# Dilated attention computed as a near part and a far part, joined per pair of heads

## The chip, the core and the metric

The program runs on one core of one Trainium2 chip. Its engines work side by side, each through its own instructions in order: TensorE (PE) multiplies matrices into PSUM banks, VectorE (DVE) and ScalarE (ACT) do elementwise work, GpSimd (POOL) splits weights, SyncE (SP) issues most DMAs. Engines wait for one another through semaphores. The metric is the device time of one execution in microseconds; lower is better.

## The reference, cut to what matters

The program is a decoder trunk of two layers at 1024 positions and width 1024, in fp32. The change touches one part of layer 0: attention with 8 heads of width 64, in which three dilated windows are mixed.

```python
DILATED_BRANCHES = ((128, 1), (512, 4), (2048, 16))   # (window, dilation)

def dilated_attention(q, k, v):
    outs = [dilated_branch(q, k, v, w, d) for (w, d) in DILATED_BRANCHES]
    ms = jnp.stack([m for _, m, _ in outs])
    ls = jnp.stack([l for _, _, l in outs])
    os_ = jnp.stack([o for o, _, _ in outs])
    wts = ls * jnp.exp(ms - jnp.max(ms, axis=0, keepdims=True))
    o = jnp.einsum('gbhs,gbhsd->bhsd', wts, os_) / jnp.sum(wts, axis=0)[..., None]
    return o
```

A branch (window w, dilation d) lets a query see the keys at distances 0, d, 2d, ... up to w, by a softmax with maximum m, sum l and output o. The mixture equals one softmax in which a key counts as often as branches see it. Keys seen by the second and third branch lie at distances that are multiples of 4, up to 1023 here.

## The kernel before

All matrices are stored with the feature on the 128 partitions and the position along the free axis. A product in fp32 is made of three products in fp32r: operands are split into a high part (a copy that rounds) and a low part (the rest), and high x high, high x low and low x high are added up. A projection of one 128-wide tile over half the positions is 8 *pieces* of three 128x512 matmuls each (L1031 to L1033; for the output projection L1074 to L1076).

The heads go in four pairs (`hp` 0 to 3; `NHP` is 4). For a pair and a tile of 128 queries (`ST` is 8 tiles) the stage does this:

- `scores` (PE, L1101): three products per head against all keys from the first to the tile's own, in chunks of 512 keys. With tile t there are t + 1 blocks of 128 keys, 36 for a pair of heads.
- `top` (DVE, L1680): adds `lmul`, the log of the number of branches that see the key (or -1e30), and takes the minimum of the negated scores. `exp` (ACT, L2239) gives the exponentials and their sum.
- `transposes` (PE, L1116) turn the blocks round by a product with the unit matrix; `take` (ACT, L2250) copies them from PSUM. `values` (PE, L1136) multiplies with V by position (`a_vn`).
- `recip`, `spread` and `recip_transpose` (DVE L1689, ACT L2258, PE L1124) bring 1/sum beside the output; `take_out` (DVE, L1695 and L1697) writes `oT`.

Steps with more than four blocks are cut in two groups. `PAIRS` is 32 pairs of a head pair and a query tile. One order is written out by hand for each engine. On PE it is: scores of the next tile, then `fill` (pieces of the projections of the next pair of heads, as `PIECES` counts them), transposes of this group, values of the group before. In the last pair of heads the fill is 6 pieces that are left and, by `WO_PIECES`, pieces of the first tile of the output projection. For these, ScalarE makes high parts of `oT` (`split_high`, L2263) where `WO_HIGHS` says, and VectorE low parts (`split_low`, L1711) where `WO_LOWS` says. Projected K and Q are rotated by `rope` on VectorE in stages (L1653 to L1668). After the last pair `residual` projects the other output tiles (L826 to L832). The normalizing of the gated linear attention (`out_step`, L1576 to L1589) still runs on VectorE beside the first pair of heads. GpSimd splits each tile of weights in two operations (L596 and L602).

Of the kernel before, what the change touches and what calls it, by code (L numbers as in the profile page):

```python
# [22 lines left out]
F32 = mybir.dt.float32  # L23
# [31 lines left out]

G_MIX0, G_MIX1, G_FFN0, G_FFN1, G_FIN, G_SGU, G_OUT, G_N = 0, 8, 16, 24, 32, 40, 48, 49
# [14 lines left out]
def constant_arrays():  # L71
# [14 lines left out]
    d = (ST - 1) * P + p[:, None] - np.arange(S)[None, :]  # L86
    count = np.zeros((P, S), np.float64)
    for window, dil in BRANCHES:
        count += (d >= 0) & (d <= window) & (d % dil == 0)
    m = np.where(count > 0, np.log(np.maximum(count, 1.0)) / A_SCALE, NEG)  # L90
    return c, m.astype(np.float32)


def build(nc, xT, pos, consts, logmul, gains, wgu, bgu, wgl, w_in, w_out, w_u, w_v, w_outc, wsT, bsp,
          w_up, w_dn, conv, outT):
    with ExitStack() as ctx:
# [56 lines left out]
        lmul = sb("lmul", 192, [P, S])  # L153
# [19 lines left out]
        a_vn = [sb("a_vn0", 88, [P, ST, P]), sb("a_vn1", scr[1], [P, ST, P])]  # L173
# [6 lines left out]
        a_sh = [sb("a_sh0", 176, [P, S]), sb("a_sh1", scr[4], [P, S]), sb("a_sh2", 136, [P, S])]  # L180
        scores_sb = sb("a_s", scr[5], [P, 3 * S])
        a_pt = sb("a_pt", 172, [P, 4, HALF])
        a_r = sb("a_r", 205, [P, P])
        a_rows = sb("a_rows", 206, [P, 2, P])
# [23 lines left out]
        s_preload = sem("copy_function_loaded")  # L208
# [25 lines left out]
        s_eps = sem("eps_written")  # L234
# [19 lines left out]
        class Asem:  # L254
            def __init__(self):
# [8 lines left out]
                self.rl = sem("a_recip_done")  # L264
                self.rb = sem("a_recip_spread")
# [3 lines left out]
                self.rt = sem("a_recip_transposed")  # L269
                self.rtf = sem("a_recip_taken")  # L270
                self.of = sem("a_out_taken")
        A = Asem()
# [171 lines left out]

        R_A = 6 * NBP
# [11 lines left out]
        def _(sp):  # L457
# [15 lines left out]
            sp.wait_ge(s_setup, 2)  # L473
# [10 lines left out]
            for hp in range(NHP):  # L484
                for t, blk in enumerate((VA + hp, KA + hp, QA + hp)):
                    plain(N_A + 3 * hp + t, w_in[blk])
# [103 lines left out]
        def _(pool):  # L590
# [39 lines left out]
            for hp in range(1, NHP):  # L630
                if hp > 1:
                    plain(N_A + 3 * hp, (N_A + 3 * hp) % 2, (s_proj, N_A + 3 * hp - 1), (A.rope, 20 * hp - 5))
                    plain(N_A + 3 * hp + 1, (N_A + 3 * hp + 1) % 2, (s_proj, N_A + 3 * hp), (A.rope, 20 * hp))
                plain(N_A + 3 * hp + 2, (N_A + 3 * hp + 2) % 2, (s_proj, N_A + 3 * hp + 1))
            plain(N_WO, 0, (s_proj, R_WO - 1), (A.rope, 20 * NHP - 5))
            plain(N_WO + 1, 1, (s_proj, R_WO), (A.s, 16 * (NHP - 1) + 14))
# [117 lines left out]
        def tile_of(n):  # L754

            return n // ST, TILE_ORDER[n // ST][n % ST]

# [1856 lines left out]
```

## Time and profile before

| | us |
|---|---|
| median of 3 runs | 2117.36 (2117.34 to 2118.32) |
| profiled execution, its own time | 2116.54 |
| its span | 2114.7 |
| TensorE busy | 2085.5 |
| VectorE busy | 1464.5 |
| ScalarE busy | 882.3 |
| GpSimd busy | 877.2 |

The profile is of one execution. Busy time of TensorE is the union of overlapping matmuls, so the length of one matmul in a row is more than its share of the time; the distance between two starts is that share. A bracket behind a row of the timeline is the idle time of the engine before it and who ended it. The pairs of heads stand in the trace from 232.06 to 294.51, to 357.51, to 416.97 and to 477.21 us: each stretch begins with the scores of the second query tile of the pair, and the last ends where the third tile of the output projection starts.

### The profile page before, as it was taken

What the parts mean: (1) busy time and instruction counts of PE and PEld (TensorE: products, weight loads), DVE (VectorE), ACT (ScalarE), POOL (GpSimd) and SP (SyncE); (2) the same over time, 40 slices, a digit from 0 to 9 for tenths busy, and PEclk for the clock granted to TensorE, in tenths of its full rate; (3) what the DMA queues carried; (4) which work ended last, traced back from release to release, by engine and by line L of the source; (5) the groups of instructions that cost most, each with busy time, mean ns of one, the idle gap of its engine ahead of it and who ended that gap; (6) DMA issues with size and microseconds to landing.
All of it is one profiled execution on the core that took longest, in us unless ns stands there. A gap on an engine that the chain in (4) does not pass through costs nothing.

```text
span 2114.7 us, 26180 instructions
## 1 busy us (share of the span) xinstructions
PE 2085.5 (99%) x10190; PEld 1706.5 (81%) x10190; DVE 1464.5 (69%) x1631; ACT 882.3 (42%) x1156; POOL 877.2 (41%) x456
## 2 busy tenths in 40 slices
PE   8999999999999999999999999999999999999997
PEld 6888777778888888888888888888788888888886
DVE  7668845554986677777889604537966676776988
ACT  4231434453554444444445421215544444454444
POOL 4322121123587767770001233434877677730000
PEclk9999999999999999999999999999999999999999
DMA  4101000021422222117984111213222221239872
GB/s 171 40 31 41 31 31 11 24 94 47 156 90 71 89 90 89 61 70 266 389 297 159 54 40 41 60 40 120 89 81 90 90 81 69 90 130 383 305 276 80
DMA packets 95164, 236.14 MB, mean 112 GB/s; under 512 B 10113, under 2 KB 12482, under 8 KB 95042
## 3 DMA queue, kind: packets, MB, share of 16 engines
q1 hardware_dynamic: 93170, 229.73, 30.6%
q10 hardware_dynamic: 1872, 4.74, 0.6%
q8 instruction: 81, 1.33, 0.3%
q14 instruction: 41, 0.34, 0.0%
HBM read 198.78 MB, written 35.65 MB: 111 GB/s over the span
## 4 chain that ended last, share of the span: by engine, by line
PE 89%; DVE 7%; issue 2%; ACT 1%; POOL 0%; DMA 0%; DVEq 0%; SPq 0%; ACTq 0%; POOLq 0%
PE ps L1231 12%; PE ps L1233 12%; PE ps L1232 12%; PE ps L1265 7%; PE ps L1268 7%; PE ps L1267 7%; PE ps L826 5%; PE ps L829 5%; PE ps L832 5%; PE ps L1031 2%; PE ps L1033 2%; PE ps L1032 2%; PE ps L1136 2%; PE ps L1101 1%; PE ps L1336 1%
## 5 line engine op out<-in xcount | busy, mean ns | idle before, releaser
L596 POOL TENSOR_TENSOR w_hi<-w_raw,ones 128x1024 fp32r<-128x1024 f32 x54 | 109.7, 2031 | 721.0 <-PE ps L832 228.1
L1231 PE MATMUL ps<-t_hi,w_hi 128*128 128x512 f32 x672 | 263.9, 393 | 1.7 <-ACT snap L2377 1.3
L1233 PE MATMUL ps<-t_hi,w_lo 128*128 128x512 f32 x672 | 261.7, 389 | 0.0
L1232 PE MATMUL ps<-t_lo,w_hi 128*128 128x512 f32 x672 | 261.5, 389 | 0.0
L1265 PE MATMUL ps<-d_hi 128*128 128x512 f32 (+1 forms) x640 | 244.7, 382 | 1.0 <-DVE d_lo L1944 1.0
L1267 PE MATMUL ps<-d_lo,d_hi 128*128 128x512 f32 (+1 forms) x640 | 243.9, 381 | 0.0
L1268 PE MATMUL ps<-d_hi,d_lo 128*128 128x512 f32 (+1 forms) x640 | 243.9, 381 | 0.0
L653 POOL TENSOR_TENSOR w_lo<-w_sum,w_hi 128x1024 fp32r<-128x1024 f32 x84 | 232.4, 2777 | 24.1 <-ACT w_hi L2380 24.1
L653 POOL TENSOR_TENSOR w_lo<-w_raw,w_hi 128x1024 fp32r<-128x1024 f32 x84 | 157.6, 1876 | 172.4 <-ACT w_hi L2380 158.7
L1231 PE MATMUL ps<-act_hi,w_hi 128*128 128x512 f32 x504 | 196.2, 389 | 0.3 <-POOL w_lo L653 0.3
L1232 PE MATMUL ps<-act_lo,w_hi 128*128 128x512 f32 x504 | 196.1, 389 | 0.0
L1233 PE MATMUL ps<-act_hi,w_lo 128*128 128x512 f32 x504 | 196.0, 389 | 0.0
L826 PE MATMUL ps<-act_hi,w_hi 128*128 128x512 f32 x592 | 184.9, 394 | 2.3 <-DVE oT L1526 1.1
L829 PE MATMUL ps<-act_lo,w_hi 128*128 128x512 f32 x592 | 182.5, 389 | 0.0
L832 PE MATMUL ps<-act_hi,w_lo 128*128 128x512 f32 x592 | 182.3, 389 | 0.0
L602 POOL TENSOR_TENSOR w_lo<-w_raw,w_hi 128x1024 fp32r<-128x1024 f32 x56 | 147.1, 2626 | 35.6 <-ACT w_hi L2278 31.3
L1231 PEld LDWEIGHTS ps<-t_hi,w_hi 128*128 128x128 f32 x672 | 126.1, 188 | 35.7 <-ACT snap L2377 10.1
L2380 ACT ACTIVATE w_hi<-w_sum 128x1024 fp32r<-128x1024 f32 x84 | 89.1, 1061 | 151.5 <-PE ps L1233 111.7
L2364 ACT ACTIVATE ps<-fz,cw 128x1024 f32<-128x1024 f32 x88 | 105.6, 1202 | 106.6 <-DVE fz L1909 100.3
L1233 PEld LDWEIGHTS ps<-t_hi,w_lo 128*128 128x128 f32 x672 | 126.1, 188 | 26.7
L1232 PEld LDWEIGHTS ps<-t_lo,w_hi 128*128 128x128 f32 x672 | 126.2, 188 | 25.6
L1901 DVE TENSOR_TENSOR fz<-ps,snap 128x512 f32<-128x512 f32 x40 | 27.7, 692 | 169.4 <-PE ps L1233 169.4
(305 smaller groups left out, 4494.0 us busy)
## 6 DMA issues: line engine op xcount, KB each, us to landing
w_raw<-w_up SPq DMA_DIRECT2D x44, 1024.0 KB, 5.0
d_ring<-w_dn SPq DMA_DIRECT2D x146, 256.0 KB, 7.9
d_ring<-g_kept SPq DMA_DIRECT2D x124, 256.0 KB, 9.3
g_kept<-gst SPq DMA_DIRECT2D x44, 512.0 KB, 2.6
w_raw<-w_in SPq DMA_DIRECT2D x24, 512.0 KB, 3.5
chain_a<-g_kept SPq DMA_DIRECT2D x44, 256.0 KB, 8.7
x_kept<-x SPq DMA_DIRECT2D x16, 512.0 KB, 7.9
x<-x_kept SPq DMA_DIRECT2D x16, 512.0 KB, 10.1
```

Of the source, the lines that this page charges most:

```text
L596: pool.tensor_tensor(w_hi[:, slot, :], w_raw[:, parity, :], ones[:, 0:1].to_broadcast([P, 1024]), ALU.mult).then_inc(s_whi, 1)
L602: pool.tensor_tensor(w_lo[:, slot, :], w_raw[:, parity, :], w_hi[:, slot, :].bitcast(F32), ALU.subtract).then_inc(s_wsplit, 1)
L653: pool.tensor_tensor(w_lo[:, slot, cols].rearrange("p (a j c) -> p a j c", j=4, c=P), src, w_hi[:, slot, cols].bitcast(F32).rearrange("p ( ...
L826: pe.matmul(out[:, cols], wh, act_hi_k[:, cols], start=first, stop=False)
L829: pe.matmul(out[:, cols], wh, act_lo_k[:, cols], start=False, stop=False)
L832: ins = pe.matmul(out[:, cols], wl, act_hi_k[:, cols], start=False, stop=last)
L1231: pe.matmul(out, wh, bh, start=(fresh and j == 0), stop=False, skip_group_check=True)
L1232: pe.matmul(out, wh, bl, start=False, stop=False, skip_group_check=True)
L1233: ins = pe.matmul(out, wl, bh, start=False, stop=(j == 3), skip_group_check=True)
L1265: pe.matmul(out, w[:, 0, wcols], w[:, 1, cols], start=(s == 0 and i not in (D6, D7)), stop=False, skip_group_check=True)
L1267: pe.matmul(out, w[:, 0, wcols], g[:, 1, cols], start=False, stop=False, skip_group_check=True)
L1268: return pe.matmul(out, g[:, 0, wcols], w[:, 1, cols], start=False, stop=(s == NBLK - 1), skip_group_check=True)
```

## The change

The attention of a pair of heads is computed in two parts. The near part is branch 1: each query tile against its own key tile and the one before it, 15 blocks. The far part is branches 2 and 3: positions are sorted by their remainder modulo 4 (their class), each class has 256 positions in two tiles, and scores within a class take 1 + 2 blocks, 12 in all for four classes. Together they make 27 blocks. A pair of heads is now `SA` = 8 steps, four near (two query tiles each) and four far (one class each), and `STEPS_A` is 32.

Each part has its own maximum, sum and unscaled output. At the end of a pair of heads the statistics of the far part, which lie by class, are moved to natural positions (`statistics_by_quadrant` on DVE, `move_statistics` on PE: four 128x32 matmuls), the two parts' factors are computed in a few small operations (`statistics_differ`, `statistics_exp`, `statistics_join`), spread by ACT to 128x512 rows four times, transposed by PE (16 transposes), and multiplied in and added by DVE (`combine_out`). This happens in the first six steps of the next pair of heads; after the last pair it stands among pieces of the output projection.

K and V are stored with positions within a tile sorted by class (VectorE writes them with a step of 32 elements, `mixed`); Q keeps its order and far scores read it with a step of 4 elements. V is transposed twice, once by tile (`a_vn`) and once by class (`a_vc`, after a copy `v_by_class` on ACT). Scores of a step go to one bank per head, two units (`u`) next to each other. The taking of the output moves from VectorE to ScalarE for all steps but the last six. The order of the projected tiles becomes K, Q, V for pairs 1 to 3, and `PIECES`, `WO_PIECES`, `WO_HIGHS` and `WO_LOWS` change. Three setup semaphores are merged.

```diff
+        def query_tiles(g):
+
+            hp, s = divmod(g, SA)
+            if s < NEAR:
+                return [(2 * s + u, range(max(2 * s + u - 1, 0), 2 * s + u + 1)) for u in range(2)]
+            return [(u, range(u + 1)) for u in range(2)]
...
-        PIECES = ((10,), (7,), (9,), (6,), (3, 3), (2, 2), (2, 2), (2, 2))
-        PIECES = (PIECES,) * 2 + (((8,), (8,), (7,), (5,), (2, 2), (2, 2), (2, 2), (2, 2)),
-                                  ((4,), (2,), (), (), (), (), (), ()))
-        WO_HIGHS = ((), (0,), (1, 2), (3,), (4,), (5,), (6,), ())
-        WO_LOWS = ((), (), (0, 1), (2,), (3,), (4,), (5,), (6,))
-        WO_PIECES = ((0,), (0,), (0,), (4,), (2, 0), (2, 0), (2, 0), (2, 2))
...
+        PIECES = ((6,) * 8, (6,) * 8, (6, 6, 6, 6, 4, 4, 4, 4), (4, 4, 0, 0, 0, 0, 0, 0))
+        WO_PIECES = (0, 0, 0, 2, 2, 2, 2, 2)
+        WO_HIGHS = ((), (), (0,), (1,), (2,), (3,), (4,), (5, 6))
+        WO_LOWS = ((), (), (0,), (1,), (2,), (3,), (4,), (5, 6))
...
+            def scores(g):
+
+                hp, s = divmod(g, SA)
+                pe.wait_ge(A.rope, 20 * hp + (10 if s < 2 else 20))
+                if g:
+                    pe.wait_ge(A.max, 4 * g)
...
+                            if s < NEAR:
+                                qs = q[rows, tile * P:(tile + 1) * P]
+                                ks = k[rows, blocks[0] * P:(blocks[-1] + 1) * P]
+                            else:
+                                qs = of_class(q[:])[rows, s - NEAR, tile * P:(tile + 1) * P]
+                                ks = by_class(k[:])[rows, s - NEAR, 0:4 * len(blocks), :]
+                            ins = pe.matmul(ps[:, 2 + h, lo:hi], qs, ks, start=(q is qh and k is kh), stop=(q is ql))
...
+            for g in range(STEPS_A):
+                hp, s = divmod(g, SA)
+                if g + 1 < STEPS_A:
+                    scores(g + 1)
+                fill(g)
+                transposes(g, 0)
+                transposes(g, 1)
+                for target, i in v_moves_of(g):
+                    v_transposes(target, i)
+                if hp and 1 <= s < 5:
+                    factor_transposes(hp - 1, s - 1)
+                if s == SA - 1:
+                    move_statistics(hp)
+                if g:
+                    values(g - 1)
...
+            for g in range(STEPS_A):
+                hp, s = divmod(g, SA)
+                if g - 2 >= SA * (NHP - 1):
+                    take_out(g - 2)
+                if hp and s == 0:
+                    statistics_differ(hp - 1)
+                if g + 1 < STEPS_A:
+                    tops(g + 1)
...
+                    if s == 0:
+                        take_part(0, Q1, (1, 2))
+                        for step_n in range(5):
+                            out_step(1, 1, step_n)
...
+                if hp == NHP - 1:
+                    if s < 2:
+                        take_part(hp, V0 + s)
+                    for kk in WO_LOWS[s]:
+                        attention_low(WO_ORDER[kk])
```

The rows below name each instruction by line, operation, written and read tiles, shape, and the semaphores it waits for. On ACT in the last pair of heads, before, around one high part: `act_hi<-oT` is the high part, `a_pt<-ps` the take of transposed blocks, `a_s,tiny<-a_s,tiny` the exponentials of one head for the next tile.

```order
L2250 ACTIVATE a_pt<-ps 128x512 [waits a_pv_done,a_transposed] x2
L2258 ACTIVATE a_rows<-tiny 128x128 [waits a_recip_transposed,a_recip_done]
L2239 ACTIVATE a_s,tiny<-a_s,tiny 128x896 [waits a_recip_done,a_max_done]
L2250 ACTIVATE a_pt<-ps 128x256 [waits a_pv_done,a_transposed] x2
L2239 ACTIVATE a_s,tiny<-a_s,tiny 128x896 [waits a_recip_done,a_max_done]
L2263 ACTIVATE act_hi<-oT 128x1024
```

After the change, at the same place (far steps; `a_class` holds their statistics):

```order
L2433 ACTIVATE a_s,a_class<-a_s,a_class 128x128 [waits a_max_done]
L2433 ACTIVATE a_s,a_class<-a_s,a_class 128x256 [waits a_max_done]
L2433 ACTIVATE a_s,a_class<-a_s,a_class 128x128 [waits a_max_done]
L2433 ACTIVATE a_s,a_class<-a_s,a_class 128x256 [waits a_max_done]
L2442 ACTIVATE a_pt<-ps 128x384 [waits a_pv_done,a_transposed] x2
L2476 ACTIVATE act_hi<-oT 128x1024
```

All exponentials of the next step now stand ahead of the takes of this one, and the high part stands behind both.

On VectorE in the last pair of heads, before: a maximum is an `ISA` row on `a_s` with its read-out behind it, `act_lo<-oT,act_hi` is the low part.

```order
L1680 ISA a_s,tiny<-ps,lmul 128x896 [waits a_exp_done,a_transposed,a_scores_ready]
L1680 ISA tiny 128x1
L1689 RECIPROCAL tiny<-tiny 128x2 [waits a_recip_spread,a_exp_done]
L1711 TENSOR_TENSOR act_lo<-oT,act_hi 128x1024 [waits wo_hi]
L1695 COPY a_r<-ps 128x128 [waits a_pv_done]
L1697 TENSOR_TENSOR oT<-ps,a_r 128x128 [waits a_recip_taken]
```

After:

```order
L1863 COPY oT<-ps 128x256 [waits a_pv_done]
L1805 ISA a_s,a_class<-ps,lmul 128x128 [waits a_transposed,a_scores_ready]
L1805 ISA a_class 128x1
L1805 ISA a_s,a_class<-ps,lmul 128x256
L1805 ISA a_class 128x1
L1805 ISA a_s,a_class<-ps,lmul 128x128 [waits a_transposed,a_scores_ready]
L1805 ISA a_class 128x1
L1805 ISA a_s,a_class<-ps,lmul 128x256
L1805 ISA a_class 128x1
L1851 TENSOR_TENSOR a_far<-ps,a_far 128x512 [waits a_out_taken,a_factor_transposed]
L1880 TENSOR_TENSOR act_lo<-oT,act_hi 128x1024 [waits wo_hi]
```

The low part now stands behind the output, four maxima and a join, and ahead of the next step's maxima. On PE after the change, from the scores of a far step of the last pair to the first piece of the output projection:

```order
L1185 MATMUL ps<-a_kh_134,a_qh_136 128x128 [waits a_max_done,a_rope_steps]
L1185 MATMUL ps<-a_kh_134,a_qh_136 128x128
L1185 MATMUL ps<-a_kl_137,a_qh_136 128x128 x2
L1185 MATMUL ps<-a_kh_134,a_ql_141 128x128 x2
L1185 MATMUL ps<-a_kh_134,a_qh_136 128x256 x2
L1185 MATMUL ps<-a_kl_137,a_qh_136 128x256 x2
L1185 MATMUL ps<-a_kh_134,a_ql_141 128x256 x2
L1154 MATMUL ps<-act_hi,w_hi 128x512 [waits wo_lo]
L1155 MATMUL ps<-act_lo,w_hi 128x512
L1156 MATMUL ps<-act_hi,w_lo 128x512
```

The piece waits for its low part; the low part that it needs is the one that VectorE makes in the step just before, where the pieces of the kernel before use one that is a tile older.

## Rows read from the trace of the kernel before

**Rows 1.** The page: busy time of an engine; engines in the chain that ended last.
```profile
PE 2085.5 (99%) x10190; PEld 1706.5 (81%) x10190; DVE 1464.5 (69%) x1631; ACT 882.3 (42%) x1156; POOL 877.2 (41%) x456
...
PE 89%; DVE 7%; issue 2%; ACT 1%; POOL 0%; DMA 0%; DVEq 0%; SPq 0%; ACTq 0%; POOLq 0%
```
**Rows 2.** Windows, one per pair of heads: length, then busy us per engine, clock, DMA.
```profile
232.06:294.51 62.45, 62.25 (x433) 49.43 (x432) 49.37 (x99) 26.60 (x67) 11.26 (x5) 1.00 0.11 31
294.51:357.51 63.00, 62.92 (x450) 50.29 (x448) 32.24 (x87) 25.43 (x67) 12.80 (x6) 1.00 0.08 26
357.51:416.97 59.46, 59.13 (x432) 46.85 (x430) 30.76 (x83) 25.65 (x67) 8.89 (x5) 1.00 0.07 23
416.97:477.21 60.24, 57.30 (x422) 44.00 (x421) 32.73 (x70) 30.89 (x70) 19.25 (x9) 1.00 0.26 95
```
**Rows 3.** Timeline of PE, second pair of heads into the third: start, length, instruction.
```profile
352.15 1.03 PE L1116 MATMUL ps<-cst,a_s 128*128 128x128 f32 x8
353.11 0.88 PE L1136 MATMUL ps<-a_pt,a_vn 128*64 128x128 f32 x12
353.92 0.50 PE L1031 MATMUL ps<-act_hi,w_hi 128*128 128x512 f32 x1
...
356.49 1.09 PE L1136 MATMUL ps<-a_pt,a_vn 128*64 128x128 f32 x16
357.51 0.39 PE L1101 MATMUL ps<-a_kh,a_qh 64*128 64x256 f32 x2
357.74 0.28 PE L1101 MATMUL ps<-a_kl,a_qh 64*128 64x256 f32 x2
357.85 0.28 PE L1101 MATMUL ps<-a_kh,a_ql 64*128 64x256 f32 x2
358.06 0.50 PE L1031 MATMUL ps<-act_hi,w_hi 128*128 128x512 f32 x1
...
361.59 0.39 PE L1031 MATMUL ps<-act_hi,w_hi 128*128 128x512 f32 x1
...
362.27 0.39 PE L1031 MATMUL ps<-act_hi,w_hi 128*128 128x512 f32 x1
```
**Rows 4.** Timeline of ACT: exponentials, takes and high parts.
```profile
240.92 0.50 ACT L2239 ACTIVATE a_s<-a_s,tiny 128x256 f32<-128x256 f32 x1
...
425.02 0.87 ACT L2250 ACTIVATE a_pt<-ps 128x384 f32<-128x384 f32 x2 [2.00 <-PE ps L1116]
...
427.39 1.05 ACT L2263 ACTIVATE act_hi<-oT 128x1024 fp32r<-128x1024 f32 x1
428.34 1.08 ACT L2250 ACTIVATE a_pt<-ps 128x512 f32<-128x512 f32 x2
...
429.90 0.40 ACT L2239 ACTIVATE a_s<-a_s,tiny 128x128 f32<-128x128 f32 x1
...
430.30 0.39 ACT L2239 ACTIVATE a_s<-a_s,tiny 128x128 f32<-128x128 f32 x1
```
**Rows 5.** Timeline of DVE: maxima, a normalizing step, a low part.
```profile
236.60 0.41 DVE L1680 CUSTOM_DVE_ANT_0 a_s<-ps,lmul 128x256 f32<-128x256 f32 x1
...
237.02 1.20 DVE L1576 SCALAR_TENSOR_TENSOR b_v<-b_v,glT 128x1024 f32<-128x1024 f32 x1
...
428.93 0.28 DVE L1680 CUSTOM_DVE_ANT_0 a_s<-ps,lmul 128x128 f32<-128x128 f32 x1
...
429.43 1.21 DVE L1711 TENSOR_TENSOR act_lo<-oT,act_hi 128x1024 fp32r<-128x1024 f32 x1
```
**Rows 6.** Timelines of POOL and DVE: a low part beside a split of weights.
```profile
451.15 2.38 POOL L602 TENSOR_TENSOR w_lo<-w_raw,w_hi 128x1024 fp32r<-128x1024 f32 x1
...
451.83 2.78 DVE L1711 TENSOR_TENSOR act_lo<-oT,act_hi 128x1024 fp32r<-128x1024 f32 x1
```
**Rows 7.** Timeline of PE in the last pair of heads.
```profile
433.04 0.50 PE L1074 MATMUL ps<-act_hi,w_hi 128*128 128x512 f32 x1 [0.64 <-DVE act_lo L1711]
```
**Rows 8.** Loads of Q as weights for the scores, over the whole stage.
```profile
L1101 PEld LDWEIGHTS ps<-a_kh,a_qh x96: 182/183/185, 225.9 to 449.5; 64*128 64x128 f32 x96
```

More of the change, by code:

```diff
@@ new lines, in build, with parts_in_order, half_done @@
+        LATER_PARTS = (K0, Q0, K1, Q1, V0, V1)
+        BANK_OF = {V0: 0, V1: 1, K0: 0, Q0: 1, K1: 0, Q1: 1}
+        def parts_in_order(hp):
+            return LATER_PARTS if hp else FIRST_PARTS
+        def half_done(hp, part):
+            order = parts_in_order(hp)
+            h = order.index(part) % 2 if part in (V0, V1) else (part - K0) // 2
+            tiles = [p for p in order if p in (V0, K0, Q0)]
+            tile = {V0: V0, V1: V0, K0: K0, K1: K0, Q0: Q0, Q1: Q0}[part]
+            return h, 3 * hp + tiles.index(tile) + 1
@@ new lines, in values @@
+            def values(g):
+                hp, s = divmod(g, SA)
+                pe.wait_ge(A.ptf, 2 * g + 2)
+                pe.wait_ge(A.vn, 5 * hp + (1 if s < 2 else 2 if s < NEAR else 5))
+                if g:
+                    pe.wait_ge(A.of, g)
+                for u, (tile, blocks) in enumerate(query_tiles(g)):
+                    lo = score_cols(g, u)[0]
+                    for i, b in enumerate(blocks):
+                        for h in range(2):
+                            rows = slice(64 * h, 64 * h + 64)
+                            v = a_vn[:, b, rows] if s < NEAR else a_vc[:, 2 * (s - NEAR) + b, rows]
+                            ins = pe.matmul(ps[rows, 7, u * P:(u + 1) * P], v,
+                                            a_pt[:, 2 * (g % 2) + h, lo + i * P:lo + (i + 1) * P],
+                                            start=(i == 0), stop=(i == len(blocks) - 1))
@@ L1657, in rope @@
                     return
-                dve.wait_ge(A.free, 6 * hp + 3 + 2 * h + is_q)
+                dve.wait_ge(A.free, part_taken(hp, part))
                 dve.wait_ge(A.rope, 5 * n + 2)
                 if stage == 1:
-                    dve.tensor_tensor(out, out, sh, ALU.add).then_inc(A.rope, 1)
+                    if n == 4:
+                        dve.wait_ge(B.o[0], 10)
+                    if is_q:
+                        dve.tensor_tensor(both, out, sh, ALU.add).then_inc(A.rope, 1)
+                    else:
+                        dve.tensor_tensor(mixed(both), in_order(out), in_order(sh), ALU.add).then_inc(A.rope, 1)
```

725 lines of the change are left out of this document (418 added, 307 removed).

## Prediction

> **What bounds the kernel now.** I read the page first: TensorE is busy for 2085.5 of 2114.7 us, and of the chain that ended last 89% is TensorE's [rows 1]. Time goes only by what TensorE executes or waits for. The change touches one stage, the attention of four pairs of heads, so next come its four pairs, cut where the scores of each one's second query tile are issued: 62.45, 63.00, 59.46 and 60.24 us, with TensorE busy for all but 0.2, 0.1, 0.3 and 2.9 us, at a granted clock of 1.00 [rows 2]. ScalarE is busy for 27 to 31 us of each and VectorE for 31 to 49. So removed TensorE work comes off the time, until something else ends last. Of a matmul's time I take the distance between starts, since busy times overlap. From the timeline [rows 3]: one piece of projection (three 128x512 matmuls) 0.68 us; eight transposes 0.96, so 0.12 each; the values of three key tiles 0.81 and of four 1.02; the six score matmuls of a 128x256 unit 0.55, of which a pair of heads in the middle costs 0.11 and the rest is start and end.
>
> **Change, TensorE's side.** One pair of heads now takes 8 steps, with 27 score blocks for 36. A step's two units of scores cost 0.55 + 3 x 0.11 = 0.88, in all 8 x 0.88 = 7.0 us. Five steps have 3 blocks and three have 4: transposes 5 x 0.72 + 3 x 0.96 = 6.5, values 5 x 0.81 + 3 x 1.02 = 7.1. V is transposed twice, 16 x 0.12 = 1.9. The joining factors: 16 x 0.12 = 1.9, none of it in the first pair's steps and two shares in the last's. The four small 128x32 matmuls on the statistics aren't in the trace; their nearest row is the transpose at 0.12, so 0.5 together, taken as 0.6 with the wait for VectorE; bounds 0.2 and 1.5 us a pair. Starting a fill costs 0.1 a step, 0.8. Sum 25.8 us, 23.9 in the first pair. The first three pairs hold 48 + 48 + 40 = 136 pieces, at 0.68 that is 92.5 us; with 23.9 + 25.8 + 25.8 = 75.5 that is 168.0. Now they take 184.9 with 138 pieces. **Gain 16.9 us**, if TensorE never waits there.
>
> **Waits in the first three pairs.** A step of six pieces is 6 x 0.68 + about 3 = 7.1 us. ScalarE's part in it is four exponentials (0.40 for 128 columns by the distance of two starts, 0.50 for 256, [rows 4]), two takes of 0.4 to 0.5, one take of the output 0.3, now and then a spread of 0.6 or a copy of V: under 6 us. VectorE has four maxima (0.28 and 0.41 less the 0.07 in which the next has begun, so 0.21 and 0.34, [rows 5]) and at most a rotated half of 3.9 and a join of 1.3: 6.5 us. Both fit, and what was two maxima a tile wide hides as before. One place doesn't fit, the start of the first pair. Scores are now taken into one bank per head, so those of step n+1 wait for all maxima of step n, and those of step 2 need the rotated Q of the whole sequence, which was wanted only at tile 4. From the maximum that starts 4.2 us into the pair, VectorE does 1.1 of maxima, 2.0 of rotation and five normalizing steps of 1.24 (the first, at 237.02, took 1.20, [rows 5]), and only then the maxima of step 2: 15.0 us in. TensorE has 5.7 us of work in step 0 and 6.9 in step 1, plus a start delayed to 7.3 us by the rotation. It would wait 1.6 and then 0.8: **2.4 us lost** (between 0 and 4, as the casts happen to meet GpSimd).
>
> **The last pair.** Here there is little projection to hide behind: 8 pieces of V and, before the loop ends, 10 of the output projection. Each of those needs an operand high (ScalarE, 0.95 us) and low (VectorE, 1.2). Before, these run a step ahead. Now, by the order of the instructions, ScalarE does exponentials of step n+1, takes of step n, high; VectorE does the output, maxima of step n+1, low; and the next fill on TensorE stands right on that low, with transposes and values queued behind it. In a round nothing overlaps in this ring: low 1.2, output 0.3, first maximum 0.25, four exponentials 1.8, two takes 0.76 (0.97 with four blocks; 0.87 and 1.08 busy less 0.1 of overlap), high 0.95, four crossings of 0.05: 5.5 us [rows 4, 5]. TensorE's own work in a round is 0.88 + 1.46 + 0.72 + 0.81 = 3.9. Laid out from the pair's start: step 0 takes 5.7 us and step 1 6.5. ScalarE, still taking V by class, ends its step 1 at 12.6, then a spread to 13.1, exponentials to 15.5, takes 16.5, two copies of V 17.5, high 18.5, low 19.8. Fills then start at 19.8, 25.4, 30.8, 36.3 and 41.7. The fourth and fifth include a low held up by GpSimd's split of output weights: such a low took 2.78 us, starting 0.7 after a GpSimd operation of 2.38 did [rows 6]. The last step has two highs and two lows before VectorE prepares the statistics, so the matmuls on these stand until 48.1 and the values after them end at 49.5. Behind that TensorE has 22 pieces, 0.8 of values and 1.9 of factors, 18.0 us without a wait, since statistics, exponential and joins (about 0.5 + 0.3 + 0.7 + 4 x 0.6) run beside 8 pieces. So 67.5 to 68 us for 60.24 now: **7.8 us lost**. Already before, a fill waited 0.64 us for act_lo in this pair, the first sign of that ring [rows 7].
>
> Moved and free: weights split in another order (K, Q, V) are waited for by pieces more than 5 us later; the take-out that moved from VectorE to ScalarE is in the steps above; three small semaphore merges cost nothing. The four exponentials a step for two are priced above; their fixed part is why ScalarE's share rises although blocks fall.
>
> **Sum.** -16.9 + 2.4 + 7.8 = -6.7 us on the profiled 2116.54 us gives 2109.8; the median of the runs is 0.8 above that one execution, so about 2110.7 us.
>
> **Rivals.** (1) The ring is hidden: ScalarE's and VectorE's queues take the steps a round ahead and the last pair costs its TensorE content, about 56 us. Then -16.9 + 2.4 - 4.2 = -18.7, 2098 us. The order of the instructions shown with the change speaks against it. Chance 0.08. (2) More waits than I see in pairs 1 to 3, where ScalarE's in-order queue (V copies that wait for values) starts exponentials late: 1 us in 8 of 24 steps, or a ring of 7 us for 5.5 if each low meets GpSimd: +6 to +9, net -1 to +2, 2115 to 2119 us. For it: VectorE is already busy 49 of 62 us in the first pair [rows 2]. Chance 0.25. (3) Slower, by one mechanism: the far scores read Q with a step of four elements, as weights for TensorE. No row of before has such an operand, so its price lies between nothing and several times the 0.11 us of a pair of heads. In the 12 far steps of pairs 1 to 3, 72 pairs of matmuls; at 0.22 each they cost 7.9 us (2118.6, no measurable change), at 0.33 they cost 15.8 and the kernel is at 2126.5. It turns slower than before by over 0.2% from 0.26 us a pair on. I take 0.11, because loading these 128 weights takes 0.18 us already [rows 8], and still a pair of heads comes every 0.11: loads overlap each other and the matmuls. Chance that it costs 0.2 or more: 0.14.
>
> The Trainium skill, page "SBUF — State Buffer", section "Door 1: The DMA port swizzle", speaks for rival 3: accesses in one 16-byte line run at full speed, and each that moves to a new line pays; a step of four fp32 puts every element of Q in a new line. It gives no price, and no row of before shows it.
>
> (4) Few things go otherwise: the order isn't what the diff says; 0.03. The forecast keeps 0.50.
>
> **Numbers.** What this kernel's measurement can tell from no change is about 0.2%, 4.2 us: faster ends at 2113.1, slower begins at 2121.6. The forecast case spreads 3.5 us to each side (statistics, the start, GpSimd) and gives faster 0.38 of its 0.50 and same 0.12. Rival 1 adds 0.08 to faster; rival 2 gives 0.03 faster, 0.17 same and, where both of its kinds add up, 0.05 slower; rival 3 0.01, 0.05 and 0.08; the rest 0.03 is split. Together faster 0.51, same 0.35, slower 0.14. Range 2103 to 2121 us: it leaves out rival 1 and the dear end of rival 3. The likeliest case alone is 2107 to 2114.
>
> **What the changed profile would show.** First three pairs: about 170 us between the same marks, with TensorE waiting under 3 us, nearly all before the scores of steps 2 and 3 of the first pair, for VectorE. Score matmuls of far steps at 0.11 us a pair of heads. Last pair: about 68 us, TensorE idle for some 13 of it, released by act_lo, in rounds of 5.5 us. After it, the same as before, 7 us earlier. I am wrong if far scores stretch, if TensorE waits for exponentials in pairs 1 to 3, or if fills of the last pair don't wait.

## The result: 2130.6 us, slower by 13.2 us

The changed kernel takes 2130.57 us (median of 4 runs, 2129.13 to 2134.45), the kernel before in the same runs 2117.35. The ratio is 1.0068, with a 95% interval of 1.0055 to 1.008. The forecast was 2110.7 us. The profiled execution took 2130.35 us.

The page of the changed kernel, busy time, beside [rows 1]:

```profile
PE 2088.0 (98%) x10166; PEld 1717.9 (81%) x10166; DVE 1476.9 (69%) x1728; ACT 905.1 (43%) x1277; POOL 875.3 (41%) x456
```

TensorE is busy for 2.5 us more than before although nine score blocks a pair of heads are gone, and the span grew by 13.8 us. The windows, cut at the same marks as [rows 2] (length, then busy time of PE, PEld, DVE, ACT and POOL, clock, DMA):

```profile
233.71:296.48 62.77, 59.92 (x417) 49.58 (x416) 49.75 (x116) 30.16 (x93) 15.43 (x7) 1.00 0.11 34
296.48:359.26 62.78, 62.29 (x446) 51.94 (x444) 34.97 (x109) 32.30 (x98) 12.81 (x7) 1.00 0.09 26
359.26:414.74 55.48, 55.48 (x412) 46.55 (x410) 31.69 (x108) 30.27 (x95) 8.93 (x5) 1.00 0.09 30
414.74:492.17 77.43, 65.55 (x436) 53.48 (x435) 37.41 (x99) 37.74 (x98) 14.07 (x7) 0.91 0.09 29
```

The first three pairs of heads take 181.0 us (before 184.9; forecast 168.0 + 2.4 = 170.4), the last 77.4 (before 60.2; forecast 68), at a mean clock of 0.91. The first mark stands 1.65 us later than before, the last 15.0 us later, and behind it 1.2 us come back. So there are two gaps to explain: 10.6 us in three pairs, and 9.4 us in one.

**Far scores.** TensorE, scores of a near step and then of a far step, each up to the next piece (the shapes of a row are stationary, then moving):

```profile
249.32 0.32 PE L1185 MATMUL ps<-a_kh,a_ql 64*128 64x256 f32 x2
249.44 0.31 PE L1185 MATMUL ps<-a_kh,a_qh 64*128 64x256 f32 x2
...
256.56 0.45 PE L1185 MATMUL ps<-a_kh,a_qh 64*128 64x128 f32 x2
256.84 0.40 PE L1185 MATMUL ps<-a_kl,a_qh 64*128 64x128 f32 x2
257.08 0.40 PE L1185 MATMUL ps<-a_kh,a_ql 64*128 64x128 f32 x2
257.31 0.46 PE L1185 MATMUL ps<-a_kh,a_qh 64*128 64x256 f32 x2
257.61 0.40 PE L1185 MATMUL ps<-a_kl,a_qh 64*128 64x256 f32 x2
257.84 0.40 PE L1185 MATMUL ps<-a_kh,a_ql 64*128 64x256 f32 x2
258.16 0.51 PE L1099 MATMUL ps<-act_hi,w_hi 128*128 128x512 f32 x1
```

A pair of heads is one row here: the same product for both heads. Near, a row starts every 0.12 us. Far, one starts every 0.24 (0.30 where the second unit begins), even where the moving operand is half as wide. A far step's scores take 258.16 - 256.56 = 1.60 us and were priced at 0.88. The loads of Q, beside [rows 8]:

```profile
L1185 PEld LDWEIGHTS ps<-a_kl,a_qh x128: 184/257/331, 227.3 to 453.6; 64*128 64x128 f32 x128
```

The shortest is 0.18 us as before, the longest 0.33.

**Statistics.** TensorE at the end of the first pair of heads:

```profile
292.91 1.36 PE L1117 MATMUL ps<-cst,a_vt 128*128 128x128 f32 x8
294.66 1.08 PE L1203 MATMUL ps<-a_quad,lmul 128*128 128x32 f32 x8 [0.39 <-DVE a_quad L1814]
295.67 0.88 PE L1237 MATMUL ps<-a_pt,a_vc 128*64 128x128 f32 x12
```

VectorE at the same place:

```profile
292.46 1.10 DVE L1756 TENSOR_TENSOR a_vt<-ps,rstd 128x512 f32<-128x512 f32 x1 [3.11 <-PE ps L1101]
293.39 1.22 DVE L1814 TENSOR_TENSOR a_quad<-a_class,lmul 128x128 f32<-128x128 f32 x1
```

The four small matmuls stand in the trace as eight and take 295.67 - 294.66 = 1.01 us. VectorE prepares them only behind its write of V, so V's transposes wait a little and they do, too: the whole step is 9.32 us long, where its other parts make 7.55. That is 1.8 us in the first two pairs, and 0.9 in the third, where no V is in the way.

**The last pair.** TensorE's longest waits in it:

```profile
435.55 0.47 PE L1154 MATMUL ps<-act_hi,w_hi 128*128 128x512 f32 x1 [1.34 <-DVE act_lo L1880]
...
448.04 0.65 PE L1154 MATMUL ps<-act_hi,w_hi 128*128 128x512 f32 x1 [1.58 <-DVE act_lo L1880]
...
461.59 0.56 PE L1154 MATMUL ps<-act_hi,w_hi 128*128 128x512 f32 x1 [2.38 <-DVE act_lo L1880]
461.95 0.63 PE L1155 MATMUL ps<-act_lo,w_hi 128*128 128x512 f32 x1
462.38 0.63 PE L1156 MATMUL ps<-act_hi,w_lo 128*128 128x512 f32 x1
...
469.62 1.92 PE L1203 MATMUL ps<-a_quad,lmul 128*128 128x32 f32 x8 [4.12 <-DVE a_quad L1814]
```

These and one of 1.74 us are the ring that was forecast. New is what follows three of them: at 461.95 a 128x512 matmul starts every 0.43 us instead of every 0.23. Windows there:

```profile
446.00:448.00 2.00, 0.45 (x4) 0.25 (x4) 2.00 (x2) 0.00 (x0) 1.92 (x2) 1.00 0.00 0
448.00:450.00 2.00, 1.96 (x5) 1.58 (x6) 2.00 (x10) 1.45 (x7) 2.00 (x1) 0.56 0.00 0
...
460.00:462.00 2.00, 0.41 (x2) 0.34 (x3) 1.69 (x2) 0.28 (x1) 0.00 (x0) 0.97 0.00 0
462.00:464.00 2.00, 2.00 (x6) 1.50 (x5) 0.06 (x1) 0.00 (x0) 0.00 (x0) 0.50 0.00 0
...
466.00:468.00 2.00, 0.00 (x0) 0.00 (x0) 1.00 (x1) 1.91 (x3) 0.00 (x0) 1.00 0.00 0
...
470.00:472.00 2.00, 2.00 (x14) 1.94 (x15) 0.00 (x0) 0.00 (x0) 0.00 (x0) 0.50 0.03 8
```

Three times TensorE stands nearly idle, and three times the granted clock is at half (1.2 GHz for 2.4) in what comes next. Behind the waits of 1.34 and 1.74 us it stays at 1.00, and 128x512 matmuls start every 0.23 us. Two low parts also took 2.81 and 2.60 us for 1.22, beside GpSimd's splits of weights, as in [rows 6]. VectorE:

```profile
445.17 2.81 DVE L1880 TENSOR_TENSOR act_lo<-oT,act_hi 128x1024 fp32r<-128x1024 f32 x1 [1.40 <-ACT act_hi L2476]
...
453.44 2.60 DVE L1880 TENSOR_TENSOR act_lo<-oT,act_hi 128x1024 fp32r<-128x1024 f32 x1 [2.68 <-ACT act_hi L2476]
```

GpSimd beside them (a second split runs from 446.98 to 450.22):

```profile
445.01 1.89 POOL L620 TENSOR_TENSOR w_hi<-w_raw,ones 128x1024 fp32r<-128x1024 f32 x1 [11.78 <-PE ps L1237]
...
452.60 2.36 POOL L626 TENSOR_TENSOR w_lo<-w_raw,w_hi 128x1024 fp32r<-128x1024 f32 x1
```

### The profile page after: what moved, and what is told of

Same layout as the page of the kernel before. It is cut to its first block, busy times and chain, and to the rows that moved or that the text cites. A ratio compares the mean times of both kernels' runs of the same rounds, so it can differ in the third digit from the quotient of the medians.

```text
span 2128.5 us, 26252 instructions
## 1 busy us (share of the span) xinstructions
PE 2088.0 (98%) x10166; PEld 1717.9 (81%) x10166; DVE 1476.9 (69%) x1728; ACT 905.1 (43%) x1277; POOL 875.3 (41%) x456
## 4 chain that ended last, share of the span: by engine, by line
PE 88%; DVE 8%; issue 2%; ACT 2%; POOL 0%; DMA 0%; DVEq 0%; SPq 0%; ACTq 0%; POOLq 0%
PE ps L1343 12%; PE ps L1344 12%; PE ps L1345 12%; PE ps L1377 7%; PE ps L1380 7%; PE ps L1379 7%; PE ps L892 5%; PE ps L895 5%; PE ps L898 5%; PE ps L1099 2%; PE ps L1101 2%; PE ps L1100 2%; PE ps L1185 1%; PE ps L1448 1%; PE ps L1449 1%
## 5 line engine op out<-in xcount | busy, mean ns | idle before, releaser
L892 PE MATMUL ps<-act_hi,w_hi 128*128 128x512 f32 x592 | 184.9, 394 | 2.3 <-DVE oT L1638 1.1
```

What stands on the lines that cost most here:

```text
L892: pe.matmul(out[:, cols], wh, act_hi_k[:, cols], start=first, stop=False)
```

## The experiments

All times stand against the kernel before on the same chip, 2116.5 to 2117.0 us in each group. One thing first: executions of one kernel differ by 3 to 7 us here (by 12 to 13 in the two woven ones), with mean clocks from 0.992 to 0.999 (0.982 to 0.989 in those two). So single profiles are read by their marks, and medians by their ratios. A profile shows one execution, which can lie some us from the median.

### Q read as neighbouring columns

```diff
-                                qs = of_class(q[:])[rows, s - NEAR, tile * P:(tile + 1) * P]
+                                qs = q[rows, tile * P:(tile + 1) * P]
```

> The changed kernel with one edit: far scores read Q as 128 neighbouring elements instead of every fourth one (the far scores are then those of other positions; the amount of work is the same). If the step of four elements in Q is what doubled a pair of heads' score matmuls (0.235 us for 0.11 in far steps), they go back to 0.11 to 0.12, the 12 far steps of the first three pairs give back 12 x 0.7 = 8 us and the last pair 1 to 3: about 10 us below the changed kernel, 2121 us. If the order of K is what costs, nothing moves: 2130 us.

Measured: 2126.55 us, ratio 1.0042 (1.0028 to 1.0056), 4 us less than the changed kernel. TensorE at the same far step, and a wait in the same pair:

```profile
256.57 0.28 PE L1185 MATMUL ps<-a_kl,a_qh 64*128 64x128 f32 x2
256.69 0.28 PE L1185 MATMUL ps<-a_kh,a_ql 64*128 64x128 f32 x2
...
265.50 0.33 PE L1185 MATMUL ps<-a_kh,a_qh 64*128 64x128 f32 x2 [1.51 <-DVE a_class L1805]
```

Its loads of Q, over the whole stage:

```profile
L1185 PEld LDWEIGHTS ps<-a_kl,a_qh x128: 184/186/189, 227.1 to 448.7; 64*128 64x128 f32 x128
```

Its windows of the first, the second and the last pair of heads:

```profile
233.51:296.60 63.09, 58.72 (x415) 47.81 (x415) 49.60 (x116) 30.18 (x93) 15.11 (x7) 0.97 0.11 34
296.60:356.49 59.89, 59.40 (x445) 49.01 (x443) 35.01 (x109) 32.33 (x98) 12.83 (x7) 1.00 0.09 28
...
409.11:488.62 79.51, 65.54 (x437) 52.81 (x435) 37.80 (x99) 38.00 (x98) 14.08 (x7) 0.87 0.09 27
```

The cause is shown: without the step the loads are back at 0.18 us and the pairs of heads at 0.12. The second pair of heads is shorter by 62.78 - 59.89 = 2.9 us, four far steps at 0.72, and the third by as much. The other two pairs give nothing. In the first, TensorE now waits 1.51 us for VectorE's maxima, and the clock falls to 0.50 behind that (0.97 over the pair), so there VectorE and not TensorE sets the pace once the far scores are cheap; in the last, the ring's waits and a clock of 0.87 take more than was saved.

### K read as neighbouring columns

```diff
-                                ks = by_class(k[:])[rows, s - NEAR, 0:4 * len(blocks), :]
+                                ks = k[rows, 0:P * len(blocks)]
```

> The changed kernel with one edit: far scores read K as one run of 128 or 256 elements instead of runs of 32 (scores are those of other positions, same amount of work). If runs of 32 in the moving operand cost the time: far pairs at 0.11 us and 10 us less. If Q's step does it: far pairs stay at 0.235 us, 2130 us.

Measured in one execution: 2129.82 us, with far pairs of heads at 0.24 us still and a far step as long as in the changed kernel, 7.37 us. K's runs of 32 elements, as moving operand, cost nothing that this trace shows.

### High parts one step earlier

```diff
-        WO_HIGHS = ((), (), (0,), (1,), (2,), (3,), (4,), (5, 6))
+        WO_HIGHS = ((), (0,), (1,), (2,), (3,), (4,), (5, 6), ())
```

> The changed kernel with one table moved: each high part of the last pair is made one step earlier, the low part stays where it is, so VectorE no longer waits for ScalarE in the step. Theory of the ring: fills of the last pair stop waiting for act_lo except where GpSimd holds a low part, statistics come 1 to 2 us earlier, TensorE's clock stays at 2.4 GHz until the statistics at least; last pair 77 to about 64 us, total about 2118 us. Rival, that the last pair is bound by ScalarE's or VectorE's amount of work: the waits move to exponentials or maxima and under 4 us are won.

Measured: 2119.24 us, ratio 1.0011 (1.0001 to 1.002). One row of numbers gives 11.3 of the 13.2 us back. In the profile, which is of its fastest execution (2115.57 us), the last pair is down from 77.4 to 64.9 us; waits for act_lo of 1.70 and 0.23 us are left, and one of 1.20 for the statistics.

### Statistics ahead of the last low parts

```diff
+                    if s == SA - 1:
+                        statistics_by_quadrant(hp)
                     for kk in WO_LOWS[s]:
                         attention_low(WO_ORDER[kk])
-                if s == SA - 1:
+                elif s == SA - 1:
                     statistics_by_quadrant(hp)
```

> The changed kernel with one order turned: in the last step VectorE prepares the statistics before the two low parts instead of behind them. The wait of 4.1 us on the statistics should fall to under 1 us, but the next pieces then wait for the same low parts, which end no earlier than 1.5 us after: 1 to 3 us won. If the low clock of 469 to 475 us is a result of that wait, another 2 to 3 us. Total 2125 to 2129 us.

Measured in one execution: 2125.71 us. The wait of 4.12 us is gone, waits of 1.31 and 1.22 us for act_lo come behind it, and the last pair takes 73.2 us.

### Both together

> The high parts stand one step earlier and the last step prepares the statistics ahead of its low parts; all that is computed stays. With the high parts early alone TensorE waited 1.70 and 0.23 us for act_lo and 1.20 us for a_quad in the last pair, and the kernel took 2119.2 us. Theory (the ring and the place of the statistics are two separate waits): the wait for a_quad goes, the two for act_lo stay, 1 us less, 2118 us, between 2117 and 2119. Rival (the low parts only come later by the time of the statistics, so the wait moves to the next fill, as it did where the order alone was changed): the same 2119.2 us, a wait of about 1 us before a 128x512 piece instead.

Measured: 2115.86 us (11 runs, 2113.31 to 2118.83), ratio 0.9996 (0.9987 to 1.0005), so no different from the kernel before within the interval. The last pair of heads:

```profile
415.17:477.09 61.92, 59.28 (x437) 48.88 (x436) 37.73 (x99) 37.20 (x98) 15.07 (x7) 1.00 0.12 35
```

The forecast of 1 us was too small: 3.4 by the medians, 3.0 by the last pair's marks, where the wait of 1.20 us has gone and with it a stretch at half clock (0.97 over the pair before, 1.00 now). This row also prices the clock. TensorE issues the same instructions as in the changed kernel and is busy for 59.28 us at a clock of 1.00, where it was busy for 65.55 at 0.91: 6.3 us of the last pair's busy time were the clock.

### High parts early, with Q whole, with plain writes, with all of it

The plain writes are

```diff
             def mixed(t):
-                return t.rearrange("p (t c a) -> p t a c", c=4, a=32)
+                return in_order(t)
```

> High parts one step earlier, and far scores read Q as 128 neighbouring columns instead of every fourth; so these scores belong to other positions, while number and sizes of all instructions stay. Each of 16 far steps has 6 pairs of heads, at 0.235 us with the step and 0.11 without, 0.75 us a step. Theory (with the ring in the last pair opened, nothing takes the saved time back; it was the ring that kept the whole-Q kernel at 4 us of gain): 12 steps x 0.75 = 9 us in the first three pairs and up to 3 in the last, so 2119.2 - 9 to -12 = 2107 to 2110 us. Rival (the other engines set the pace of far steps in the first three pairs too, so most of the time is waited for instead): 2119.2 - 4 = 2115 us, with TensorE waits of 0.5 us and more for a_class or a_pt in those pairs.

> High parts one step earlier, and VectorE writes V and the sum of K without the step of 32 elements, in the order of positions; so the far part pairs wrong positions, while number and sizes of instructions stay. Such a write took 1.06 us for 512 columns and 0.69 without the step, 16 of them in the stage, 6 us of VectorE's time. Theory (VectorE is not what TensorE waits for in the first three pairs but at the start of the first): 0.5 to 1 us less than 2119.2, 2118.5 us. Rival (VectorE's length sets part of the pace of these steps): 3 us or more less, 2116 us or below.

> All four at once: high parts one step earlier, statistics ahead of the low parts in the last step, Q read as neighbouring columns in the far scores (other positions), V and the sum of K written without a step (wrong order). Theory (the effects add up, since each belongs to another place): 2119.2 - 1 - 9 to -12 - 0.7 = 2106 to 2109 us, and the first three pairs of heads take 170 us between the marks of 2110.7's prediction. Rival (they overlap: what one gives the next wait takes): 2112 us or above.

Measured: 2110.56 us with Q whole (0.9964, 0.9951 to 0.9978), 2116.42 with plain writes (0.9998, 0.9988 to 1.0007), 2107.00 with all (0.9954, 0.9938 to 0.9969). So Q's step costs 8.7 us by the medians once the ring is open. Four far steps at 0.72 in three pairs would make 8.6, but the marks don't bear this out pair by pair, and the agreement is partly chance. By the marks it is 2.9 in the second and third pair each, and nothing in the last, 64.8 us for 64.9: a wait of 3.15 us for act_lo has taken the place of 1.70 and 0.23. In the first pair it is nothing by itself, 63.1 us for 62.8 (again a wait of 1.51 us for the maxima and half clock behind it), and 2.2 together with the plain writes (60.7), with which that wait is gone. The 2.8 us of the plain writes alone are not shown: the intervals overlap (1.0001 to 1.002 without them), and the marks show 1.3 us in the last pair and none elsewhere. The version with all four takes 173.1 us for the first three pairs, not 170: the statistics are still in it.

### K and V in the order of positions, K read with a step

With both orders mended and the plain writes:

```diff
-    d = P + p[:, None] - np.concatenate([c4, P + c4])[None, :]
+    d = P + p[:, None] - np.arange(2 * P)[None, :]
...
-                                ks = by_class(k[:])[rows, s - NEAR, 0:4 * len(blocks), :]
+                                ks = of_class(k[:])[rows, s - NEAR, 0:P * len(blocks)]
...
-                act.activation(a_vcls[hp > 0].rearrange("p (c t a) -> p c t a", c=4, a=32), by_class(a_vt[hp > 0][:]), ACT.Copy
+                act.activation(a_vcls[hp > 0].rearrange("p (c j) -> p c j", c=4), of_class(a_vt[hp > 0][:]), ACT.Copy
```

> High parts early, statistics ahead of the low parts (2115.9 us so far), and K and V are kept in the order of positions: VectorE writes them without a step, the near mask is in the order of positions, far scores read K with a step of four elements as the moving operand, and ScalarE reads V with a step of four for its copy by class. All is computed. Theory (the step costs TensorE time only in the operand that it loads as weights, so K read with a step is free; VectorE's shorter writes give back what the plain writes gave before, 2.8 us, nearly all in the first pair of heads): 2113 us, pairs of heads in far scores still at 0.235 us. Rival (a step of four is dear in either operand): each pair of heads in 12 + 4 far steps goes to 0.3 us or more, 6 x 0.07 x 16 = 7 us lost, 2120 us or above.

Measured: 2116.31 us, ratio 1.0 (0.9991 to 1.0009), no better than without it. VectorE's writes of V in the kernel with the step (count, busy us, mean ns):

```profile
L1756 DVE TENSOR_TENSOR a_vt<-ps,rstd 128x512 f32<-128x512 f32 x8 | 8.7, 1088 | 11.6 <-PE ps L1101 11.2 <-issue 0.2
```

And in this one:

```profile
L1756 DVE TENSOR_TENSOR a_vt<-ps,rstd 128x512 f32<-128x512 f32 x8 | 5.5, 692 | 11.5 <-PE ps L1101 11.2 <-issue 0.2
```

They are 0.40 us shorter each, but far steps grew from 7.37 to 7.48 us, by 0.02 us for each of six pairs of heads. Neither theory holds: K's step of four, as moving operand, is not quite free, but it costs far less than the 0.12 us a pair of heads of Q's step in the weights.

### Far scores woven into the pieces

With both orders mended. In the first three pairs of heads one 128x512 matmul stands ahead of each pair of far scores:

```diff
+                    for _ in half_tile_parts(target, part, k):
+                        next(score, None)
...
+                if g + 1 < STEPS_A and (g + 1) % SA >= NEAR and hp < NHP - 1:
+                    woven(g)
+                else:
```

> High parts early, statistics ahead of the low parts (2115.9 us so far), and in the first three pairs of heads each pair of far score matmuls stands behind a 128x512 matmul of the projection instead of in one run of twelve. All is computed, Q is still read with a step. Theory (what a step in Q makes longer is the load of the weights, 0.33 us for 0.18, and a load runs beside the matmul before it; a 128x512 matmul takes 0.23, so most of the load hides behind it): of 0.72 us lost a far step 0.4 to 0.7 comes back, 12 x = 5 to 8 us, 2108 to 2111 us. Rival (the load takes a port that the running matmul needs, or it does not start before that one has ended): nothing comes back, 2116 us; or, since scores are complete 1.3 us later and VectorE's maxima with them, new waits of TensorE for exponentials, 2117 to 2119 us.

Measured: 2162.08 us, ratio 1.0221 (1.0199 to 1.0244), 46 us slower than without. TensorE in a far step:

```profile
256.29 0.50 PE L1103 MATMUL ps<-act_hi,w_hi 128*128 128x512 f32 x1
256.72 0.45 PE L1208 MATMUL ps<-a_kh,a_qh 64*128 64x128 f32 x2
257.11 0.50 PE L1105 MATMUL ps<-act_lo,w_hi 128*128 128x512 f32 x1
257.54 0.45 PE L1208 MATMUL ps<-a_kl,a_qh 64*128 64x128 f32 x2
```

One window inside the first three pairs, which take 224.7 us here (233.43 to 458.12) and 181.9 without the weaving:

```profile
228.00:430.00 202.00, 198.65 (x1129) 148.38 (x1129) 105.30 (x298) 85.46 (x260) 34.61 (x16) 0.91 0.08 24
```

A 128x512 matmul and a pair of heads together take 0.82 us, where side by side in runs they take 0.23 + 0.24. Nothing is won, and a round loses 0.35 us. Six such rounds lose 2.1 us, twelve steps 25. Most of the rest is the clock, at 0.91 over these 202 us (18 us), although TensorE shows hardly any idle time there. A round has two changes between an operand of 128 rows and one of 64. If they are all of the loss, each costs about 0.18 us; this is argued and not shown, since loads of the two kinds were not tried apart. The Trainium skill, page "TensorEngine Tiling (Array Packing)", section "Key Properties", says that a change of tiling mode drains TensorE; the 0.82 us a round for 0.47 in this trace agree. Both theories missed it, and so did the one for the run that combined it with the other edits:

> Both of the above at once (scores woven in, K and V in the order of positions), and in the first three pairs the statistics are prepared ahead of V's second half on VectorE. All is computed. In two pairs TensorE waited 0.4 us for them and came to them 0.4 us after that half's write; 0.8 us a pair at most is to be had. Theory (the effects add up): 2115.9 - 2.8 - 5 to 8 - 1 to 1.6 = 2104 to 2107 us, faster than the kernel before by 0.5%. Rival (weaving gives nothing): 2112 us.

Measured: 2166.09 us, ratio 1.0225 (1.0204 to 1.0246).

### Useless work in the idle places

The changed kernel as it is, with matmuls whose results nobody reads:

```diff
+            FILLER = (0, 0, 0, 0, 0, 6, 6, 8)
...
+                    pe.matmul(ps[:, bank, :], w_hi[:, N_WO % 2, 0:P], act_hi[:, WO_ORDER[0], 0:HALF], start=True, stop=True)
...
+                        keep_busy(6, 16)
                     move_statistics(hp)
```

> The changed kernel as it is (2130.6 us), with useless work in TensorE's idle places of the last pair of heads: 6, 6 and 8 matmuls of 128x512 behind the scores in its steps 5 to 7 and 16 ahead of the matmuls on the statistics, at 0.23 us 8.2 us of work where it stood idle for 1.6, 1.7, 2.4 and 4.1 us. Their results are overwritten; all else is computed as before. Theory (the granted clock fell to 0.50 at 448, 462 and 470 us because TensorE had stood idle just before, and this made the same instructions take 65.6 us of busy time where they took 59.3 in the kernel without idle): with the filler the clock stays at 1.00 and the kernel gets faster although it does more, by 4 to 6 us, 2125 to 2127 us. Rival (the clock falls for another reason, or its fall was hidden by the waits): 2130 us or more, by up to 2 us where a filler outlasts the wait.

Measured: 2125.79 us, ratio 1.004 (1.0026 to 1.0055): 8.2 us of work more, and 4.8 us less time. The windows in which the changed kernel's clock was at 0.56 and 0.50:

```profile
448.00:450.00 2.00, 1.98 (x9) 1.31 (x9) 2.00 (x5) 0.09 (x1) 1.92 (x2) 1.00 0.00 0
...
462.00:464.00 2.00, 2.00 (x13) 1.75 (x12) 0.00 (x0) 1.43 (x3) 0.00 (x0) 1.00 0.00 0
```

TensorE's statistics, which waited 4.12 us, wait 0.53, and the windows from 460 to 476 us are all at 1.00. So the idle times made the clock fall in these places. The mean clock of whole executions rises from 0.993 to 0.995 in the changed kernel to 0.996 to 0.998. But the clock does not stay at 1.00 everywhere, as the theory had it. A place without a filler:

```profile
435.29 0.47 PE L1154 MATMUL ps<-act_hi,w_hi 128*128 128x512 f32 x1 [1.35 <-DVE act_lo L1892]
...
436.60 0.63 PE L1155 MATMUL ps<-act_lo,w_hi 128*128 128x512 f32 x1
437.03 0.63 PE L1156 MATMUL ps<-act_hi,w_lo 128*128 128x512 f32 x1
```

Here, and behind the 1.62 us wait at 240.22, matmuls start every 0.43 us, where the changed kernel had the same waits (1.34 and 1.63 us) and kept 0.23.

### The best version

Even with the ring open, a clock fall was left in some executions. In the kernel with both orders mended, the scores of the third step waited 1.62 us, and then:

```profile
242.00:244.00 2.00, 2.00 (x7) 1.53 (x7) 1.96 (x2) 0.00 (x0) 0.00 (x0) 0.62 0.00 0
```

In the changed kernel the same wait of 1.63 us was followed by a clock of 1.00. In the traces of all runs, in this stage, the eleven waits of 1.98 to 4.18 us are each followed by half clock; of those from 1.3 to 1.8 us some are and some are not. The last version fills that place and the one in the last pair, and prepares the statistics ahead of V's second half in all pairs:

```diff
+                if g == 1:
+                    keep_busy(7, (N_A + half_done(1, K0)[1] - 1) % 2, 0, 6)
...
+                if g == STEPS_A - 2:
+                    pe.wait_ge(A.ptf, 2 * (g - 1) + 1)
+                    keep_busy(transposed_bank(0), N_WO % 2, WO_ORDER[0], 6)
...
+                if hp < NHP - 1 and s == SA - 1:
+                    statistics_by_quadrant(hp)
```

> High parts early and statistics ahead of the low parts (2115.9 us so far), the statistics also ahead of V's second half in the other pairs, and useless 128x512 matmuls in the two idle places that are left: six ahead of the scores of the third step of the first pair of heads (1.6 us idle there), six ahead of the first piece in step 6 of the last (1.7 us). All is computed. Theory (in part of the executions the clock falls to 0.5 for some 3 us after such an idle time, and TensorE never has to wait there for long): the clock stays at 1.00 all through the stage, 1.5 to 3 us less with 1 us for the statistics, 2113 us, and a narrower spread, 0.998 of the kernel before. Rival (these falls cost nothing, since they lie beside waits): the statistics' 1 us alone or nothing, 2115 to 2116 us.

Measured: 2112.97 us (11 runs, 2110.85 to 2114.93), ratio 0.9982 (0.9973 to 0.9991), 3.9 us faster than the kernel before. The spread is 4.1 us, for 5.5 without the fillers. Its first and last pair of heads:

```profile
232.82:294.93 62.11, 61.02 (x421) 50.58 (x420) 48.89 (x116) 30.13 (x93) 14.77 (x7) 1.00 0.11 34
412.55:474.43 61.88, 60.83 (x443) 49.90 (x441) 37.75 (x99) 37.20 (x98) 15.04 (x7) 1.00 0.12 36
```

The step with the statistics went from 9.32 to 8.66 us, in two pairs, and no window of the stage is below full clock. The last pair takes as long as without its filler (61.88 us for 61.92, where the clock was at 1.00 too). Fillers and statistics were not tried apart, so the 2.9 us between the two medians are not divided up. Q's dear loads are still in it. A copy of Q sorted by class should remove them; this was not tried.

## Why the prediction was wrong, step by step

**Pieces, transposes, values, other engines in pairs 1 to 3: right in the second and third.** With Q whole the second pair takes 59.9 us; the forecast for it was 48 x 0.68 + 25.8 = 58.4, and 1.2 of the difference is the statistics. TensorE waits for nothing in the third pair. In the first it was wrong, though the changed kernel hides it: with far scores near the forecast price TensorE waits 1.51 us for VectorE's maxima, which the forecast did not have, and the pair takes 63.1 us, not 58.9. Rival 2 named VectorE's load in that pair as its reason.

**Price of the far scores: wrong, the largest miss.** The forecast took 0.11 us a pair of heads because loads overlap. They do at 0.18 us each, but not enough at 0.33. Measured 0.235; 12 steps x 0.72 = 8.6 us of TensorE's time. Taking it away gave 5.8 us by the marks, since in the first pair VectorE takes over. Rival 3 had this mechanism and priced it at 7.9 us for 0.22. The row it was judged by, [rows 8], shows loads of contiguous columns only and could not speak for a step. The Trainium skill's rule on 16-byte lines ("SBUF — State Buffer", section "Door 1: The DMA port swizzle"), cited there with a chance of 0.14, was the better witness: K's runs of 32 were free in the one execution, a step of four in the weights was not.

**Statistics: mis-sized.** 0.6 us a pair with bounds of 0.2 and 1.5; measured 1.8, 1.8 and 0.9, because the four fp32 matmuls take 1.01 us (the trace shows eight) and VectorE has V in the way. That is 2.7 us more than forecast. With the far scores it makes 11.3 us; 1.0 goes off since half of V's transposes, counted in the third pair, fall in the last, and 0.3 is left of the 10.6.

**Start of the first pair: right.** Forecast waits of 1.6 and 0.8 us; measured 1.63 and 0.73, for a_ql and a_stat.

**The ring of the last pair: right in kind, its rounds too short.** Forecast some 13 us idle and the statistics 48.1 us into the pair; TensorE was idle for 77.43 - 65.55 = 11.9 us. But the statistics came at 54.9. The forecast's rounds are 5.4 to 5.6 us each, with a low part of 1.2. It says that two of them include a low part held up by GpSimd, but has no time for it. Measured from first piece to first piece they are 5.5, 7.0, 8.1 and 5.5 us: the second and third hold the low parts of 2.81 and 2.60 us, 3.0 us more together, and the third begins at half clock. The waits nearly match in sum because the work between them grew too, so this match is partly luck. The forecast had 68 - 13 = 55 us of TensorE's work. The kernel with both orders mended shows 59.3 at full clock: 2.9 of that are far scores, 1.0 the V transposes moved here, 0.3 the statistics.

**The clock: not in the prediction at all.** It was put at nothing and made TensorE busy for 6.3 us more. The forecast read 1.00 in all four windows of [rows 2] and carried it over, though it put 13 us of idle time into a pair of heads whose longest wait had been 0.86. In the sum, 55 + 4.3 + 6.3 + 11.9 = 77.5 us, which divides up the measured 77.4. The Trainium skill, page "TensorE: Matmul & The Clock Gate", section "What's actually happening", says that the clock is set by how busy TensorE was before, that its low level follows idle time, and that where a change of level falls varies from run to run; a fall behind 1.62 us in one trace and none behind 1.63 in another agree.

So two steps failed: the price of a far pair of heads, 0.11 us for a measured 0.235, and the clock, taken as 1.00 for a measured 0.91 in the last pair. The sizes of the statistics and of two rounds of the ring come behind them.

Not explained: the first mark stands 1.65 us later than before, where the other versions have it 0.6 to 1.7 us later.

## What to carry to other kernels

A sum of idle times is not their cost: where TensorE will stand still for longer than anywhere in the trace at hand (0.86 us before, 1.3 to 4.1 us after), price what follows at half clock as well, or fill the place with matmuls whose results nobody reads. When matrices are re-sorted, ask for each operand which role it has: here runs of 32 were free as moving operand, and a step of four cost 0.02 us a pair of heads there and 0.12 as weights. And ask what takes over when a dear operand is made cheap: in the first pair of heads it was VectorE, and nothing was won there. And where a stage loses its cover of projection work, look first at the order of the small operations that feed it; one row of numbers was worth 11 us here.

## What the hardware showed that was not expected

- Weights of 64 rows by 128 columns of fp32r: 0.18 us contiguous, 0.33 with a step of four elements.
- VectorE writing 512 columns with a step of 32 elements: 1.09 us for 0.69.
- Four 128x32 matmuls in fp32 take 1.01 us, 0.25 each, and stand as eight in the trace.
- 64-row and 128-row matmuls alternating: 0.82 us for 0.47, and a clock of 0.91 with TensorE busy for 198.65 of 202 us.
- 36 useless matmuls in TensorE's waits made a kernel 4.8 us faster.
- The same wait, 1.34 or 1.35 us, was followed by half clock in one trace and by full clock in another.
